# Block one's final norm and block two's first norm taken from one pair of sums, the context's half of that norm moved beside an earlier product, and modulation chunks regrouped

## The reference

```python
def _rmsnorm(x, w):
    return x * rsqrt(mean(x * x) + EPS) * w

def first_block(...):
    ...
    h = h + _conv_ffn(_rmsnorm(h, ffn_norm_w[l]), ffn_up[l], ffn_conv_w[l], ffn_down[l])
    return _rmsnorm(h, final_norm_w)

def adaln(cvec, w_mod, b_mod):
    m = silu(cvec) @ w_mod + b_mod          # nine vectors of 1024 per layer
    ...
def modulated_norm(x, g, shift, scale):
    return rms_norm(x, g) * (1 + scale) + shift

def ffn_half_step(x, mods, g, w_gu, w_down):
    shift, scale, gate = mods
    return x + 0.5 * gate * swiglu(modulated_norm(x, g, shift, scale), w_gu, w_down)
```

## Time and profile before

| | |
|---|---|
| median of 3 timed runs | 2292.48 us (2286.9 to 2300.02) |
| the profiled execution, its own time | 2289.85 us |
| its span | 2287.7 us |
| TensorE matmuls busy | 2136.4 us (93% of the span) |
| VectorE busy | 1002.8 us (44%) |
| ScalarE busy | 788.3 us (34%) |
| GpSimd busy | 221.4 us (10%) |
| loads | 314.22 MB, 137 GB/s on the mean |

### The profile page before, as it was taken

How to read it: one execution, slowest core, us unless ns; L and a number is a source line. 1 busy time by engine, 2 the same in 40 slices (tenths; PEclk the granted TensorE clock), 3 DMA queues, 4 the chain that set the end, 5 groups by cost and what they waited for, 6 DMA issues and landing times.

```text
span 2287.7 us, 30872 instructions
## 1 busy us (share of the span) xinstructions
PE 2136.4 (93%) x13478; PEld 1809.4 (79%) x13479; DVE 1002.8 (44%) x1284; ACT 788.3 (34%) x965; POOL 221.4 (10%) x184
## 2 busy tenths in 40 slices
PE   6988898999899999999989999899998998989997
PEld 5975887998678888878768888776886886848997
DVE  6667545667442332353452232234222234645454
ACT  5641444545332222232232222223211223444443
POOL 1000000313101001100001101110100111001101
PEclk9998999999899999999999999999999999999999
DMA  6425564454742222242342232324234223353453
GB/s 225 146 75 185 190 254 172 158 188 169 255 161 85 94 107 84 94 179 74 113 164 89 86 111 91 123 99 184 75 100 154 89 76 110 111 221 133 172 188 108
DMA packets 53686, 314.22 MB, mean 137 GB/s; under 512 B 5936, under 2 KB 12080, under 8 KB 23728
## 3 DMA queue, kind: packets, MB, share of 16 engines
q1 hardware_dynamic: 51360, 309.50, 38.0%
q10 hardware_dynamic: 2192, 2.75, 0.4%
HBM read 311.18 MB, written 1.05 MB: 136 GB/s over the span
## 4 chain that ended last, share of the span: by engine, by line
PE 86%; DVE 7%; DMA 3%; ACT 2%; issue 1%; SPq 0%; POOL 0%; DVEq 0%; ACTq 0%
PE psum L235 26%; PE psum L236 26%; PE psum L237 25%; DMA raw<-in_mod 3%; PE psum L1539 2%; DVE w_lo L219 2%; PE psum L1241 1%; ACT w_hi L211 1%; PE psum L1219 1%; PE psum L956 0%; DVE work L386 0%; PE psum L1233 0%; PE psum L325 0%; PE psum L1639 0%; PE psum L1640 0%
## 5 line engine op out<-in xcount | busy, mean ns | idle before, releaser
L235 PE MATMUL psum<-xn_hi,w_hi 128*128 128x256 f32 (+1 forms) x2504 | 845.4, 338 | 26.5 <-DVE xn_lo L379 11.2
L236 PE MATMUL psum<-xn_lo,w_hi 128*128 128x256 f32 (+1 forms) x2504 | 839.7, 335 | 0.0
L237 PE MATMUL psum<-xn_hi,w_lo 128*128 128x256 f32 (+1 forms) x2504 | 839.0, 335 | 0.0
L219 DVE TENSOR_TENSOR w_lo<-raw,w_hi 128x2048 fp32r<-128x2048 f32 (+1 forms) x246 | 509.3, 2071 | 426.3 <-ACT w_hi L211 425.6
L235 PEld LDWEIGHTS psum<-xn_hi,w_hi 128*128 128x128 f32 x2504 | 481.4, 192 | 84.9 <-issue 35.2
L236 PEld LDWEIGHTS psum<-xn_lo,w_hi 128*128 128x128 f32 x2504 | 481.3, 192 | 46.9 <-issue 0.7
L237 PEld LDWEIGHTS psum<-xn_hi,w_lo 128*128 128x128 f32 x2504 | 480.9, 192 | 46.6
L211 ACT ACTIVATE w_hi<-raw 128x2048 fp32r<-128x2048 f32 (+1 forms) x246 | 421.7, 1714 | 221.2 <-PE psum L237 168.4
L235 PE MATMUL psum<-h_hi,w_hi 128*128 128x512 f32 (+1 forms) x880 | 306.8, 349 | 1.8 <-POOL h_lo L1514 1.8
L236 PE MATMUL psum<-h_lo,w_hi 128*128 128x512 f32 (+1 forms) x880 | 306.2, 348 | 0.0
L237 PE MATMUL psum<-h_hi,w_lo 128*128 128x512 f32 (+1 forms) x880 | 306.0, 348 | 0.0
(11 more groups left out here) (333 smaller groups left out, 1347.7 us busy)
## 6 DMA issues: line engine op xcount, KB each, us to landing
raw<-in_mod SPq DMA_DIRECT2D x72, 1024.0 KB, 4.8
raw<-in_a_up SPq DMA_DIRECT2D x42, 1024.0 KB, 4.8
raw<-in_b_up SPq DMA_DIRECT2D x42, 1024.0 KB, 4.8
raw<-in_ffn_up SPq DMA_DIRECT2D x22, 1024.0 KB, 4.9
raw<-in_a_down SPq DMA_DIRECT2D x32, 704.0 KB, 4.0
raw<-in_b_down SPq DMA_DIRECT2D x32, 704.0 KB, 4.1
raw<-in_ffn_down SPq DMA_DIRECT2D x16, 704.0 KB, 4.2
raw<-in_wo SPq DMA_DIRECT2D x8, 1024.0 KB, 4.9
```

Source lines behind the costliest of these rows:

```text
L219: dve.tensor_tensor(w_lo[:, slot, 0:size], raw[:, raw_slot(("main", g)), 0:size], w_hi[:, slot, 0:size].bitcast(F32), ALU.subtract).then_i ...
L235: pe.matmul(out, lh, rh, start=first, stop=False, skip_group_check=group)
L236: pe.matmul(out, lh, rl, start=False, stop=False, skip_group_check=group)
L237: return pe.matmul(out, ll, rh, start=False, stop=last, skip_group_check=group)
```

## The change

Six things are changed.

1. **One pair of sums for two norms.** With u = the residual h after feed0 and w the final gain, x1 = u w / sqrt(mean(u²) + EPS). The mean of x1² is mean(u² w²) / (mean(u²) + EPS). `FinalNorm` squares each tile of the residual twice (with and without the gain, side by side in 512 columns of `nrm`), sums both at once, and builds the reciprocal root for both halves: `C` for the final norm, `X` for the modulated one, whose mean of squares carries EPS times the other. Its scale column `joint` is the product of both gains (`final_gains`). `between` goes, and so does the separate squaring of `n20`.
2. **The residual later.** `dve_residual` writes x1 into `xc` after `n20`'s high and low parts are made.
3. **The context's half by itself.** `ContextNorm` (`n20c`) does the norm of the context: squares on ScalarE after the seventh up chunk of feed0, adds on GpSimd, sums on TensorE ahead of the first down product of feed0, stats on VectorE ahead of it, and scale, high and low of one tile beside each chunk of that down product.
4. **The second group of columns** is turned and taken ahead of feed0's first down product, not at its half.
5. **Chunks regrouped.** Of the third group of twelve, before: three ahead of `ffn_down1`, nine ahead of `a1_up0`. After: three each ahead of `ffn_up1`, `a1_up0`, `a1_up1` and `a1_down1`.
6. **The third group's rows and columns** come later: rows out at the late hook of feed1, turned after the second chunk of `a1_down1`, columns taken after feed1 on VectorE, ahead of `n21`.

The diff, without the reshaping of `Norm.dve_scaled` into `dve_scale` and `dve_low` (the same instructions in the same order):

```diff
-MODS_DURING = dict(w_out=12, wv=3, wq=3, wo=3, ffn_up0=3, ffn_down1=3, a1_up0=9, ab_a=3, ...)
+MODS_DURING = dict(w_out=12, wv=3, wq=3, wo=3, ffn_up0=3, ffn_up1=3, a1_up0=3, a1_up1=3, a1_down1=3, ab_a=3, ...)
...
 # Feed.pe
+                    if not half and before_down is not None:
+                        before_down()
+                    pe_feature_major(pe, down, h_hi, h_lo, slice(0, self.w), n_tiles=1, k_tiles=HALF, before_k=hidden_k,
+                                     after_chunk=after_down if half else None)
...
 # Feed.act
+                        if not half and s.c == 6 and within_up is not None:
+                            within_up()
                     run_act(act, job, evac, splits=self.conv is None)
-                    run_act(act, jobs[f"{self.name}_down{half}"], then.act_squares_after(act) if half else None)
+                    if not half and before_down is not None:
+                        before_down()
+                    run_act(act, jobs[f"{self.name}_down{half}"], then if half else beside_down)
...
 # Feed.dve
+                    def add_and(s):
+                        add(s)
+                        if not half and beside_down is not None:
+                            beside_down(s)
+                    if not half and before_down is not None:
+                        before_down()
+                    run_dve(dve, jobs[f"{self.name}_down{half}"], add_and)
...
 # Feed.pool
+                        if not half and s.c == 8 and within_up is not None:
+                            within_up()
...
+        class ContextNorm(Norm):
+            def act_squares(self, act):
+                act.wait_ge(ctx_in, 16)
+                act.wait_ge(n_lo, ffn.split_base + KT)
+                for k in range(0, KT, self.tiles):
+                    act.activation(nrm[:, k:k + self.tiles, 0:T], xc[:, k:k + self.tiles, C], ACT.Square).then_inc(n_sq, 1)
+
+        class FinalNorm(Norm):
+            def __init__(self, scale, shift):
+                super().__init__(X, scale, shift)
+                self.w = 2 * T
+            def act_squares_after(self, act):
+                def evac(s):
+                    act.wait_ge(evacuated, s.g + 1)
+                    act.activation(nrm[:, s.c, 0:T], xc[:, s.c, X], ACT.Square, scale=col("final_norm_w", s.c)).then_inc(final_sq, 1)
+                    act.activation(nrm[:, s.c, T:2 * T], xc[:, s.c, X], ACT.Square).then_inc(n_sq, 1)
+                return evac
+            def dve_stats(self, dve):
+                m, r, j3 = mean[:, :], rstd[:, :], 3 * self.j
+                tmp = work[:, 7168:7168 + 2 * T]
+                dve.wait_ge(n_sum, self.j + 1)
+                dve.tensor_scalar(m[:, C], psum[:, 6, C], 1.0 / D, EPS, ALU.mult, ALU.add).then_inc(final_mean, 1)
+                dve.wait_ge(final_mean, 1)
+                dve.scalar_tensor_tensor(m[:, X], m[:, C], D * EPS, psum[:, 6, X], ALU.mult, ALU.add).then_inc(n_mean, 1)
+                # then guess and Newton step on all 512 columns, as in Norm
+            def dve_residual(self, dve):
+                for k in range(KT):
+                    dve.scalar_tensor_tensor(xc[:, k, X], xc[:, k, X], col("final_norm_w", k), rstd[:, C], ALU.mult, ALU.mult).then_inc(final_x, 1)
+
+        def final_gains(dve):
+            w = small[:, cols["final_norm_w"]:cols["final_norm_w"] + KT]
+            dve.scalar_tensor_tensor(joint, scales[:, 0, :, 0], D ** 0.5, w, ALU.mult, ALU.mult).then_inc(final_scale, 1)
+            dve.wait_ge(final_scale, 1)
...
-        between = Norm(X, lambda k, h: col("final_norm_w", k), out=xc[:, :, X])
-        n20, n21 = modulated(0, XC, direct=5), modulated(1, XC)
+        n20c = ContextNorm(C, lambda k, h: scales[:, 0, k, 1:2], lambda k, h: mods[:, k, 1:2], tiles=4, direct=4)
+        n20 = FinalNorm(lambda k, h: col("joint", k), lambda k, h: mods[:, k, 0:1])
+        n21 = modulated(1, XC)
...
 # TensorE
-            feed0.pe(pe, lambda: mod_turn(pe), lambda: mods_pe(pe, 3))
-            between.pe(pe)
-            mods_pe(pe, 4)
+            def context_sums():
+                mod_turn(pe)
+                n20c.pe(pe)
+            feed0.pe(pe, lambda: mods_pe(pe, 3), before_down=context_sums)
+            pe.wait_ge(final_sq, KT)
             n20.pe(pe)
-            mods_pe(pe, 5)
-            feed1.pe(pe, lambda: mod_turn(pe))
+            mods_pe(pe, 3)
+            feed1.pe(pe, lambda: mods_pe(pe, 3), lambda: mods_pe(pe, 3), within_down=lambda: mod_turn(pe))
...
 # ScalarE
-            feed0.act(act, between)
-            between.act_rest(act)
-            act.wait_ge(ctx_in, 16)
-            for k in range(KT):
-                act.wait_ge(n_scaled, between.scaled_base + k + 1)
-                act.activation(nrm[:, k, :], xc[:, k, :], ACT.Square).then_inc(n_sq, 1)
+            feed0.act(act, n20.act_squares_after(act), within_up=lambda: n20c.act_squares(act), before_down=lambda: n20c.act_guess(act),
+                      beside_down=lambda s: n20c.act_high(act, range(s.c, s.c + 1)))
...
 # VectorE
-            feed0.dve(dve, lambda: mod_columns(dve))
-            between.dve(dve)
+            def context_stats():
+                mod_columns(dve)
+                n20c.dve_stats(dve)
+                final_gains(dve)
+            def context_tile(s):
+                n20c.dve_scale(dve, s.c)
+                if s.c:
+                    n20c.dve_low(dve, s.c - 1)
+            feed0.dve(dve, lambda: n20c.dve_low(dve, KT - 1), None, context_stats, context_tile)
             n20.dve(dve)
-            mod_rows_out(dve)
-            feed1.dve(dve, lambda: mod_columns(dve))
+            n20.dve_residual(dve)
+            dve.wait_ge(final_x, KT)
+            feed1.dve(dve, None, lambda: mod_rows_out(dve))
+            mod_columns(dve)
...
 # GpSimd
-            feed0.pool(pool)
-            between.pool(pool)
+            feed0.pool(pool, lambda: n20c.pool(pool))
```

More of the change, by code:

```diff
@@ L369, in dve_scaled @@
             def dve_scaled(self, dve, tiles):
-                r = rstd[:, 0:self.w]
[L372 to L388, removed]
@@ L389, in dve_scaled, with dve_scale @@
-                if self.out is None and not self.pool_low:
-                    low(KT - 1)
+                for k in tiles:
+                    self.dve_scale(dve, k)
+                    if self.out is None and k and not self.pool_low:
+                        self.dve_low(dve, k - 1)
+                if self.out is None and not self.pool_low:
+                    self.dve_low(dve, KT - 1)
+            def dve_scale(self, dve, k):
+                r = rstd[:, 0:self.w]
+                for h in range(self.halves):
+                    t, o = slice(h * T, (h + 1) * T), slice(self.span.start + h * T, self.span.start + (h + 1) * T)
+                    dve.scalar_tensor_tensor(self.dst(k, t), xc[:, k, o], self.scale(k, h), r[:, t], ALU.mult, ALU.mult).then_inc(n_scaled, 1)
@@ new lines, in dve_low @@
+            def dve_low(self, dve, k):
+                dve.wait_ge(n_hi, self.split_base + (k + 1) * self.halves)
+                for h in range(self.halves):
+                    t, o = slice(h * T, (h + 1) * T), slice(self.span.start + h * T, self.span.start + (h + 1) * T)
+                    if self.shift is None:
+                        dve.tensor_tensor(xn_lo[:, k, o], nrm[:, k, t], xn_hi[:, k, o].bitcast(F32), ALU.subtract).then_inc(n_lo, 1)
+                    else:
+                        dve.scalar_tensor_tensor(xn_lo[:, k, o], self.dst(k, t), self.shift(k, h), xn_hi[:, k, o].bitcast(F32),
+                                                 ALU.add, ALU.subtract).then_inc(n_lo, 1)
@@ L1416, in __init__, with pe, after_down @@
                 Feed.chunks += FF_TILES
-            def pe(self, pe, halfway=None, late=None):
+            def pe(self, pe, halfway=None, late=None, before_down=None, within_down=None):
+                def after_down(c):
+                    if c == 1 and within_down is not None:
+                        within_down()
                 for half in range(2):
@@ L1501, in dve, with pool @@
                         late()
[L1502 to L1504 removed]
+                    add = dve_add_gated(dve, 1, self.gate, self.w // T)
+                    def add_and(s):
[5 more added lines that the diff above has]
+                    run_dve(dve, jobs[f"{self.name}_down{half}"], add_and)
+            def pool(self, pool, within_up=None):
                 for half in range(2):
@@ L1590, in gate_of @@
+        final_sq, final_mean, final_x, final_scale = (sem(x) for x in ("final_squares", "final_mean", "final_residual", "final_scale"))
+        joint = small[:, cols["joint"]:cols["joint"] + KT]
+        def final_gains(dve):
+            w = small[:, cols["final_norm_w"]:cols["final_norm_w"] + KT]
+            dve.scalar_tensor_tensor(joint, scales[:, 0, :, 0], D ** 0.5, w, ALU.mult, ALU.mult).then_inc(final_scale, 1)
+            dve.wait_ge(final_scale, 1)
         def gate_of(ln):
@@ L2452 @@
```

(2 more changed lines are left out.)

29 lines of the change are left out of this document (18 added, 11 removed).

## The result

The changed kernel takes 2309.03 us (median of 4 runs), the kernel before 2290.47 us on the same chips: ratio 1.0076, with a 95% interval of 1.0056 to 1.0096. It is slower by some 17 us. That lies in the predicted range and on the predicted side; the forecast was 2304. Of the changed kernel's four runs, two took 2305.3 and 2305.8 us at a mean granted clock of 0.970 and two 2312.3 and 2315.2 at 0.965, and the profiled one is the 2312.3.

A forecast was written before the change was run, and what follows sets the result against it. The prediction took TensorE as the bound, 86% of the chain. Its terms summed to +13.7 us on the profiled 2289.85, giving 2303.6, predicted as 2304 us; 8 in 10 reach from 2291 to 2314.

The forecast's parts named there:

- half of `ffn`, to the start of the second up product: Joint sums, context norm and three late chunks start up1 at 514.5 instead of 499.6: +14.9 us.
- behind it: Half-clock matmuls after the idle stretch at the half of `ffn`: +2.0 us.
- boundary, with half-clock matmuls: Between `ffn`'s last down product and `a1`'s first up product: 14.0 us against 30.9, so −16.9.
- The groups: Three-chunk groups in `a1`, third load waiting for a late split: 10.0 us at the half, 9.8 before second down product.
- The first ring: `ffn`'s first down product: ScalarE and VectorE need 4.19 us per chunk, TensorE waits 0.45 per chunk from chunk 4.
- The second ring: `ffn`'s second down product: two squares per chunk make ScalarE and VectorE's cycle 4.07 to 4.16 us, TensorE's 3.74.
- The half-clock terms: Losses to half-clock matmuls: +2.0 us behind `ffn`'s half, 1.5 at the boundary, 2.2 and 1.1 in `a1`.
- The boundary's price: Before `a1`'s first up product: 30.9 us in the kernel before, from nine chunks, two sets of sums, load waits, half clock.
- Squares and adds for the context: In an up chunk of `ffn`, in ScalarE's and GpSimd's idle time: taken at nothing; uncovered, 0 to 2 us.
- The rings do bind: Rival that they don't: extra ScalarE work hides in slack, `ffn`'s half and the boundary shorter, +5.8, 2296 us; chance 0.22.
- The groups don't hide: Rival that they do: a group's third chunk waits for nothing, 29 us less, −15, 2275 us; chance 0.07.
- collision of GpSimd with VectorE: Rival: GpSimd's adds hold up VectorE's splits in `ffn`'s products, +5.7 us, with clock losses 22.4, 2312 us; chance 0.11.

The follow-up runs named there:

- e3: The changed kernel with one modulation chunk moved from the half of `a1` (three to two) to the boundary (three to four); ratio 1.0049 against the kernel before.
- e4: The changed kernel, in `a1` VectorE splits the next job's second chunk before the last result's work at two uncovered places; ratio 0.9996 against the kernel before.
- e5: The changed kernel with ScalarE doing its work on a tile one chunk later in both down products of `ffn`; ratio 1.0048 against the kernel before.
- e11: The changed kernel with one small Silu on ScalarE behind the first down product of `ffn`; ratio 1.0040 against the kernel before, one run.
- e1: The changed kernel with chunks grouped as before: three ahead of `ffn`'s second down product, nine ahead of `a1`'s first up product; ratio 1.0033 against the kernel before.
- e2: The kernel before with only the chunks regrouped as in the changed kernel and the third group's columns after `a1`, old norms kept; ratio 1.0058.
- e9: The changed kernel with both old norms, ScalarE's tile work one chunk later, early splits and smaller chunk groups; ratio 0.9935 against the kernel before.
- e8: The kernel before with VectorE's early split alone: the next job's second chunk before the last chunk's work, where no norm follows; ratio 0.9955.

## Why the prediction was right, by its steps

| step | predicted, us | in the trace, us |
|---|---|---|
| half of `ffn`, to the start of the second up product | +14.9 | +15.6 |
| behind it | +2.0 | +3.1 |
| second down product of `ffn`, late group gone | −10.0 | −8.9 |
| boundary, with half-clock matmuls | −16.9 | −17.4 |
| two groups in `a1` | +23.1 | +22.4 |
| columns ahead of `n21` | +0.6 | +0.6 |
| sum | +13.7 | +15.4 |

- **The groups**, the step that decides: shown. 10.1 us at the half of `a1` and 9.8 ahead of its down product, 10.0 and 9.8 predicted. e3 and e4 show the mechanism from two sides: without the third chunk, and with its load released earlier. The load was taken as measured, 4.8 us. The fit that the prediction quotes beside it, of the Trainium skill's page "DMA: Bandwidth & Descriptors", section "Anatomy of one DMA", is stated there for DMAs issued from GpSimd; these are issued by SyncE.
- **The first ring**: 4.20 us, predicted 4.19; the split of chunk 2 starts at 478.06, 3.06 us after its predicted time, and 2.9 of that is the offset with which the stretch begins. e5 shows that it binds. But TensorE's own chunk lasts 3.9 us in this product and not 3.74, so three of its chunks start 0.16 to 0.22 us late, from the sixth on, where I had 0.45 per chunk from the fifth. The product is 32.2 us for a predicted 31.6.
- **The second ring**: 4.12 (601.50 to 605.62 on ScalarE), predicted 4.07 to 4.16. But it falls behind TensorE more slowly than I had it, since TensorE's chunk in this product lasts 3.90 and not 3.74. So the last square ends 3.2 us after TensorE, not 4.8, and the boundary is 11.4 rather than 12.5; the product itself is 1.2 us longer. The two nearly cancel, and that is luck.
- **The table load**, missed. I had counted the context norm's work on ScalarE, not that its reciprocal root puts out the Silu's table in the middle of the feed. The row 528.67 shows 1.28 us of it, two chunks later TensorE waits 1.46, and e11 removes that. The Trainium skill's page "ScalarE: Activation LUTs", section "What ACT_TABLE_LOAD costs", gives about 1283 ns for the load; the trace agrees with 1.28 us. The page adds about 1380 ns of drain to every switch; here the load starts 0.02 us behind the instruction before it and the next starts 0.01 us behind the load, so no such drain is seen. The wait is half of the term behind the half of `ffn`; the rest is half clock.
- **The half-clock terms** are right in sum and not one by one. Behind the half of `a1` 0.9 us were lost for a predicted 2.2, in its second down product 1.5 for 1.1, and behind the boundary 2.1 for 1.5, with 0 in e4 and e11. That they add up is luck too.
- **The boundary's price** was right in sum, but e1 corrects its reading. I took the gain as one of the norms. With nine chunks the joint norm gains 0.7 us there; with three it is 23.4 us long with the old norms (e2) and 11.4 with the new. The new norms alone shorten it by 0.7 us and the smaller group alone by 6.2, the two together by 18.2: fewer chunks expose the norm, and the shorter norm needs fewer chunks.
- **Squares and adds for the context** in the up product, taken at nothing: the two squares take 1.99 us in ScalarE's idle time, and the up product is 67.9 us before and after.
- **The rivals.** The rings do bind, so that rival falls. The groups don't hide. No collision of GpSimd with VectorE shows in the second ring, whose period is what its parts add up to; its price of 5.7 us isn't there. The exclusive hold that the Trainium skill's page "SBUF — State Buffer", section "SBUF: two separate sides", states is seen at all 22 `h_lo` of `ffn`, in both kernels alike: each starts beside a `split_lo` and ends 0.58 to 0.61 us behind that split's end, so it lasts 2.26 to 2.28 us beside a wide split and 1.59 or 1.60 beside a narrow one.
- From +15.4 in the stretch to about 17.4 by the ratio, 2 us are not accounted for; the interval, 12.8 to 22.0, holds both.

## What to carry to other kernels

Where a stream of side loads shares slots with the main loads, ask of each load which instruction releases its slot, and what stands ahead of that instruction on its engine. A group of three cost 10 us and a group of two 1.9 at the same place, and splitting the chunk ahead of the adds on VectorE took 11 us out of two such places. Before a norm is shortened, ask whether the loads beside it would end later; before work is put into a pipeline with little slack, add up its ring, with each handover from engine to engine.

## What the runs showed that was not expected

**The spacing of matmuls differs between like products.** Windows of two down products of `ffn` in e9, 15 us each: 134 matmuls of 256 columns in the first and 130 in the second, at full clock and without waits, 0.113 and 0.117 to 0.118 us apart.

```profile
480.00:495.00 15.00, 15.00 (x134) 15.00 (x134) 8.21 (x9) 5.54 (x4) 0.00 (x0) 1.00 0.73 259
580.00:595.00 15.00, 15.00 (x130) 15.00 (x129) 7.97 (x9) 6.76 (x8) 2.96 (x4) 1.00 0.69 227
```

In the kernel before, both products run at 0.113, in the changed one and in e5 both at 0.117, and in e8, which changes VectorE's order alone, only the second is slow. Within a product the spacing is the same in every chunk that doesn't wait. It costs 1.0 to 1.3 us per product, so about 2 of the changed kernel's 15.5 us. The cause is open; no run here was made for it.

**Loads reach 320 GB/s** over 29 us with three slots (e1's boundary), and then each three chunks take 9.6 us (627.74 to 637.34 in e1). A single one takes 4.8 us to be usable.
